# Gate and up projections: four instead of three of the eight step pairs by Strassen's scheme, with three buffers for the pre-added weights and three load slots

## What is computed

```
h2 = rms_norm(x, g_ffn[i])
x = x + (jax.nn.silu(h2 @ w_gate[i]) * (h2 @ w_up[i])) @ w_down[i]
```

## Time and profile before

| | |
|---|---|
| median of 3 runs | 2746.8 us (2746.69 to 2747.99) |
| the profiled execution | 2746.42 us |
| its span in the trace | 2744.6 us |
| PE / PEld busy | 99% / 83% of the span |
| DVE / ACT / POOL busy | 67% / 51% / 4% |
| pairs of gate and up | 11, between about 1930 us and 2573 us of the span |

### The profile page before, as it was taken

The page is one execution under the profiler, slowest core; times in us unless marked ns, Lnnn a source line. Parts: engine busy times, 40 slices in busy tenths (PEclk is TensorE's granted clock), DMA queues, the critical chain, the costliest instruction groups (busy, mean ns, idle before and its releaser), DMA issues.

```text
span 2744.6 us, 31158 instructions
## 1 busy us (share of the span) xinstructions
PE 2730.5 (99%) x12990; PEld 2269.2 (83%) x12990; DVE 1842.4 (67%) x1666; ACT 1405.0 (51%) x1532; POOL 110.3 (4%) x160
## 2 busy tenths in 40 slices
PE   9999999999999999999999999999999999999999
PEld 7888778888888888888888888888888888888887
DVE  5445765455468878878788685665787478658665
ACT  5435664345566556455465545344654355445553
POOL 0000000000000000000000000000121021001000
PEclk9999999999999999999999999999999999999999
DMA  7745036655545555555555664546888588768555
GB/s 235 224 148 169 32 108 200 199 184 199 175 163 206 193 199 179 204 197 193 209 185 183 225 197 145 183 156 204 257 266 252 176 252 247 246 192 255 196 182 171
DMA packets 235645, 534.16 MB, mean 195 GB/s; under 512 B 11683, under 2 KB 22513, under 8 KB 234609
## 3 DMA queue, kind: packets, MB, share of 16 engines
q1 hardware_dynamic: 218528, 486.97, 52.7%
q0 software_dynamic: 16800, 44.97, 6.7%
q10 hardware_dynamic: 176, 0.23, 0.0%
HBM read 530.03 MB, written 2.10 MB: 194 GB/s over the span
## 4 chain that ended last, share of the span: by engine, by line
PE 87%; DVE 1%; ACT 1%; DMA 0%; issue 0%
PE acc L876 13%; PE acc L877 13%; PE acc L881 13%; PE acc L1359 7%; PE acc L1360 7%; PE acc L1364 7%; PE tb L1364 7%; PE tb L1359 7%; PE tb L1360 7%; PE tb L1349 1%; PE tb L861 1%; PE acc L1142 0%; PE tb L1193 0%; ACT prob L1935 0%; PE acc L1084 0%; PE acc L1081 0%
## 5 line engine op out<-in xcount | busy, mean ns | idle before, releaser
L2326 DVE TENSOR_TENSOR wlo<-raw,whi 128x2048 fp32r<-128x2048 f32 (+2 forms) x465 | 1024.0, 2212 | 586.2 <-ACT whi L1692 585.4
L1692 ACT ACTIVATE whi<-raw 128x2048 fp32r<-128x2048 f32 (+2 forms) x465 | 858.4, 1853 | 607.9 <-PE acc L881 300.8
L876 PE MATMUL acc<-whi,ahi 128*128 128x512 f32 (+1 forms) x1456 | 566.6, 390 | 0.4 <-DVE alo L2441 0.4
L877 PE MATMUL acc<-whi,alo 128*128 128x512 f32 (+1 forms) x1456 | 562.2, 387 | 0.0
L881 PE MATMUL acc<-wlo,ahi 128*128 128x512 f32 (+1 forms) x1456 | 357.7, 387 | 0.0
L876 PEld LDWEIGHTS acc<-whi,ahi 128*128 128x128 f32 x1456 | 274.0, 188 | 55.6 <-DVE wlo L2438 0.9
L877 PEld LDWEIGHTS acc<-whi,alo 128*128 128x128 f32 x1456 | 274.1, 188 | 54.4
L881 PEld LDWEIGHTS acc<-wlo,ahi 128*128 128x128 f32 x1456 | 271.0, 188 | 55.5
L1359 PE MATMUL acc<-whi,ff_hi 128*128 128x512 f32 x512 | 201.6, 394 | 0.2 <-DVE h L2404 0.2
L1360 PE MATMUL acc<-whi,ff_lo 128*128 128x512 f32 x512 | 199.7, 390 | 0.0
L1706 ACT ACTIVATE whi<-tsum 128x1024 fp32r<-128x1024 f32 x97 | 103.1, 1062 | 182.5 <-DVE tsum L2337 122.5
(11 more groups left out here) (414 smaller groups left out, 3782.1 us busy)
## 6 DMA issues: line engine op xcount, KB each, us to landing
raw<-in_w_ff SPq DMA_DIRECT2D x128, 1024.0 KB, 5.0
raw<-in_w_in SPq DMA_DIRECT2D x119, 1024.0 KB, 5.1
raw<-in_w_gate SPq DMA_DIRECT2D x88, 512.0 KB, 4.7
raw<-in_w_down SPq DMA_DIRECT2D x44, 1024.0 KB, 5.3
raw<-in_w_up SPq DMA_DIRECT2D x55, 512.0 KB, 6.8
tpre<-in_w_up POOLq DMA_DIRECT2D x99, 256.0 KB, 5.9
raw<-in_w_out SPq DMA_DIRECT2D x16, 1024.0 KB, 5.2
raw<-in_w_o SPq DMA_DIRECT2D x16, 1024.0 KB, 5.1
```

What stands on the lines that cost most here:

```text
L876: nc.tensor.matmul(out_(t), hi[:, kt, tt(t)], whi[:, slot, wc(k)], start=first and k == 0, stop=False)
L877: nc.tensor.matmul(out_(t), lo[:, kt, tt(t)], whi[:, slot, wc(k)], start=False, stop=False)
L1692: nc.scalar.activation(whi[:, g % SPLIT, 0:n_], raw_of(n)[:, 0:n_], ACT.Copy).then_inc(w_hi, 1)
L2326: V.tensor_tensor(wlo[:, g % SPLIT, 0:n_], raw_of(load_of(g))[:, 0:n_], whi[:, g % SPLIT, 0:n_].bitcast(F32), ALU.subtract).then_inc(w_lo, 1)
```

## The change

The plan of a pair becomes D D S S D S S D. The items are then D0 D1 B2 T3 B4 T5 D6 B7 T8 B9 T10 D11. The places of the two transposes stay at steps 4 and 6, now ahead of D6 and of B9. The buffers `tpre` become three; the third one takes the place of load slot 4, so the loads have slots 0, 1 and 3. POOL's order becomes: copies of sums 0 and 1; then for each n: wait for the copies of n, the two accumulating transfers of n, and then, when the buffer is free (`wlo` of sum n-1, which used it), the copies of n+2. Each buffer gets a semaphore pair of its own.

```diff
-FF1_PLAN, FF2_PLAN, GUD_PLAN = "DDSDDSDD", "DDSDDSDD", "DDSDSDSD"
+FF1_PLAN, FF2_PLAN, GUD_PLAN = "DDSDDSDD", "DDSDDSDD", "DDSSDSSD"
...
-            double(GUD_PLAN, (0, 1, 3, 4), 2)
+            double(GUD_PLAN, (0, 1, 3), 2)
         mark["gud_end"] = len(kinds)
-        plain(4 * pairs, (0, 1) if n == len(GUD_PAIRS) - 1 else (0, 1, 3, 4))
+        plain(4 * pairs, (0, 1) if n == len(GUD_PAIRS) - 1 else (0, 1, 3))
...
-        tpre = [sb("tpre0", [P, 2, COLS], F32, W_AT + 8 * KB), sb("tpre1", [P, 2, COLS], F32, B_AT + 27 * KB)]
+        tpre = [sb("tpre0", [P, 2, COLS], F32, W_AT + 8 * KB), sb("tpre1", [P, 2, COLS], F32, B_AT + 27 * KB),
+                sb("tpre2", [P, 2, COLS], F32, W_AT + 50 * KB)]
...
-                            if n >= 2:
-                                pool.wait_ge(w_lo, SUM_ITEM[GUD_SUMS + n - 2] + 1)
-                            pool.dma_start(into[:, 0, :], wu[:, 2 * step, at]).then_inc(pre_in, 16)
-                            pool.dma_start(into[:, 1, :], wg[:, 2 * step + 1, at]).then_inc(pre_in, 16)
-                            pool.wait_ge(pre_in, 32 * (n + 1))
-                            for k in range(2):
-                                pool.dma_start(into[:, k, :], wu[:, 2 * step + 1, at], accum_op=ALU.add
-                                               ).then_inc(pre_sum, 16)
...
+                def copied(n):
+
+                    at, step = steps[n]
+                    if n >= 3:
+                        pool.wait_ge(w_lo, SUM_ITEM[GUD_SUMS + n - 3] + 1)
+                    pool.dma_start(tpre[n % 3][:, 0, :], wu[:, 2 * step, at]).then_inc(pre_in[n % 3], 16)
+                    pool.dma_start(tpre[n % 3][:, 1, :], wg[:, 2 * step + 1, at]).then_inc(pre_in[n % 3], 16)
+
+                copied(0)
+                copied(1)
+                for n, (at, step) in enumerate(steps):
+                    pool.wait_ge(pre_in[n % 3], 32 * (n // 3 + 1))
+                    for k in range(2):
+                        pool.dma_start(tpre[n % 3][:, k, :], wu[:, 2 * step + 1, at], accum_op=ALU.add
+                                       ).then_inc(pre_sum[n % 3], 16)
+                    if n + 2 < len(steps):
+                        copied(n + 2)
```

More of the change, by code:

```diff
@@ L501, in build @@
         mm_half, w_hi_half = sem("mm_half"), sem("w_hi_half")
-        pre_in, pre_sum = sem("pre_in"), sem("pre_sum")
+        pre_in, pre_sum = ([sem(f"{name}{n}") for n in range(3)] for name in ("pre_in", "pre_sum"))
         t_sum, t_hi, f_in, f_sum = sem("t_sum"), sem("t_hi"), sem("f_in"), sem("f_sum")
@@ L827, in _ @@
                 pool.wait_ge(mm_done, MARK["gud"] - 3)
[L828 to L833, removed]
-                            if n >= 2:
-                                pool.wait_ge(w_lo, SUM_ITEM[GUD_SUMS + n - 2] + 1)
-                            pool.dma_start(into[:, 0, :], wu[:, 2 * step, at]).then_inc(pre_in, 16)
-                            pool.dma_start(into[:, 1, :], wg[:, 2 * step + 1, at]).then_inc(pre_in, 16)
-                            pool.wait_ge(pre_in, 32 * (n + 1))
-                            for k in range(2):
-                                pool.dma_start(into[:, k, :], wu[:, 2 * step + 1, at], accum_op=ALU.add
-                                               ).then_inc(pre_sum, 16)
-                            n += 1
+                wg, wu = ktiles(a["w_gate_2"]), ktiles(a["w_up_2"])
+                steps = [(slice(c * COLS, (c + 1) * COLS), step) for c in range(sum(GUD_PAIRS))
+                         for step, kind in enumerate(GUD_PLAN) if kind == "S"]
+                def copied(n):
[13 more added lines that the diff above has]
+                        copied(n + 2)
                 pool.wait_ge(w_lo, MARK["gud_end"])
@@ L1701, in sums_hi @@
                         act.wait_ge(mm_done, g + 1 - SPLIT)
-                        act.wait_ge(pre_sum, 32 * (m + 1))
-                        src = tpre[m % 2][:, :, :].rearrange("p k n -> p (k n)")
+                        act.wait_ge(pre_sum[m % 3], 32 * (m // 3 + 1))
+                        src = tpre[m % 3][:, :, :].rearrange("p k n -> p (k n)")
                     else:
@@ L2334, in weight_sums @@
                 m = n - GUD_SUMS
-                pre = t[:, 0:2 * COLS] if m < 0 else tpre[m % 2][:, :, :].rearrange("p k n -> p (k n)")
+                pre = t[:, 0:2 * COLS] if m < 0 else tpre[m % 3][:, :, :].rearrange("p k n -> p (k n)")
                 if m < 0:
@@ L2341, in weight_sums @@
                 else:
-                    dve.wait_ge(pre_sum, 32 * (m + 1))
+                    dve.wait_ge(pre_sum[m % 3], 32 * (m // 3 + 1))
                     V.tensor_tensor(t[:, col(2)], pre[:, col(1)], r[:, col(1)], ALU.add).then_inc(t_sum, 1)
```

## The result

The changed kernel took 2756.3 us (median of 6 runs, 2751.35 to 2759.08), the kernel before 2747.4 in the same session (2746.69 to 2748.44). The ratio is 1.0032 [1.0022, 1.0042]: slower by 0.32%, or 8.9 us. I had forecast 2740.8. The time lies inside the range, on the other side of no change.

What follows compares the result with a forecast made beforehand. PE alone, busy for 99% of the span, was taken to set the time. From the median 2746.8 us, -7.5 for fewer matmuls and +1.5 for the first pair gave -6.0: 2740.8 us, range 2739.0 to 2757.

Steps and rivals of the forecast that it cites:

- PE's gain: One D becomes an S in each of 11 pairs: 33 matmuls less at 0.227, 7.5 us saved.
- Loads with three slots: Load of the next pair's D1: 8.7 us allowed, 9.6 in the earlier trace; a loss of 0.9 a pair or none.
- rival 2: D1's load late by 0.3 to 0.9 in eight pairs: 2743.2 to 2748.0 us; chance 0.30 together with Rival 4.
- Last step: D11, a pair's last step: `wlo` done at 36.65, needed at 36.7; no loss taken, or 0.1 to 0.3 in eight pairs.
- The walk: Step-by-step timing of ACT and DVE through one pair against PE's needs; slacks of 1.1, 1.3 and under 0.1 us.
- The first pair: Activation tiles among its weights make T5, T10 and D11 late: between nothing and 3.9 us, 1.5 taken.
- The sums by transfer: POOL's copies and accumulations for T10 land by 29.1, DVE wants them at 29.5: covered by 0.4 us.
- Rival 4: Third buffer does nothing, accumulations waiting behind copies; 0.6 a pair if 1 us later; chance 0.30 together with rival 2.
- What the transfers cost: DMA in a pair: 39.7 us needed of 41.77, 95%; 276 GB/s wanted against 281 at a share of 0.97.
- rival 3: Transfers become the bound in every pair: 0.8 to 1.2 more each, +8 to +15, 2755 to 2762 us; chance 0.30.
- a pair over 42.45 throughout: Sign: pairs that all last longer than the 42.45 us of before would mark rival 3.
- rival 2 or 3: Sign: PE waiting for the folds L2831 or L2834 would mean one of these two, a late load of D1.

Runs made afterwards that it cites:

- e10: e2 with PE making four instead of two matmuls in a pair's last step before the first one with `wlo`; 2741.35 us, ratio 0.9977.
- e1: Changed kernel with DVE making a pair's last two folds ahead of the `wlo` of the next pair's D1; 2743.92 us, ratio 0.9988.
- e2: Changed kernel with four load slots again and all three `tpre` buffers, the third in two separate halves; 2744.01 us, ratio 0.9989.
- e7: Changed kernel whose accumulating transfers add only 64 of the 512 columns; 2744.19 us, ratio 0.9986.
- e9: e1 with PE making four instead of two matmuls in a pair's last step before the first one with `wlo`; 2741.54 us, ratio 0.9980.
- e11: Kernel before with PE making four instead of two matmuls in a pair's last step before the first one with `wlo`; 2748.09 us, ratio 1.0002.
- e4: Kernel before with only the new plan: two buffers, four load slots, POOL's old order; 2793.93 us, ratio 1.0176.

## Why the prediction was wrong

**PE's gain: right.** -7.5 us from 33 matmuls at 0.227. With both waits removed (e10) a pair lasts 41.80, where 41.77 was forecast, and 6.4 of the 7.5 us arrive.

**"Loads with three slots": the step that failed.** It found the place (the slot freed by T10's sum, L2831 behind D1's `wlo`), the allowance of 8.7 us, and a landing of 9.6 in the earlier trace rows; the sum then took no loss for it, and rival 2 took at most 0.9 a pair. Measured from issue to ACT's start in the eight places: 7.5 to 10.9 us, over 8.7 in five. PE waited in six of eight, 0.24 to 2.02 us, 7.4 in all; with restarts and slow matmuls 10.6. Two things were left out. The one landing in the earlier trace rows was taken as the bad end, though the plan changes what flies beside the load: now copies and accumulations for the S steps of the next pair. And the price of a wait was taken as its own length alone. Shown by e1 (the order alone), e2 (the slot alone) and e7 (the accumulations alone).

**"Last step. Slack under 0.1 ... I take 0": mis-sized.** The walk said 0, or 0.1 to 0.3 if its sums were short. It measured 0.28 a pair (0.17 of waiting and 0.11 at the restart), 3.1 us in 11: DVE started that `wlo` 1.72 us before PE's step in e2, where the walk had 1.95 (36.3 less 34.35); e9 and e10 give 2.6 and 2.9 of it back, and e11 shows that the old plan had slack there.

**"The first pair": mis-sized the other way.** 1.5 us were taken. From its first matmul to its bank copy it lasted 36.95 us, against 37.46 before; less three matmuls that would be 36.78, so under 0.2 was lost to there, and its last step waited 0.36 longer than the others: some 0.5 in place of 1.5.

**The sums by transfer: right.** ACT waited for `tpre` four times, 3.8 us in all, and PE never for a T step's `whi`. POOL's order works against its own look-ahead as described, yet the 0.4 us of cover held well enough. Rival 4 fell with it; e4 shows what the buffer does: 37.6 us with this plan.

**What the transfers cost: the load was right, the limit was not.** 95% was forecast; the pair of e10 shows a share of 0.94. But 281 GB/s at 0.97 was no ceiling: 322, 340 and 348 GB/s stand in the windows above, at shares of 1.00 to 1.07. The trace of the kernel before had shown it, in windows that the prediction did not read:

```profile
1925.00:1935.00 10.00, 10.00 (x44) 7.99 (x43) 6.64 (x4) 3.38 (x3) 1.77 (x2) 1.00 1.06 362
1965.00:1975.00 10.00, 10.00 (x46) 8.26 (x45) 9.86 (x7) 6.69 (x7) 1.81 (x3) 1.00 1.04 346
```

The Trainium skill, "DMA: Bandwidth & Descriptors", section Specifications, puts HBM's limit for a core at about 358 GB/s. Of the windows shown here one is just past it and the others are under it, so the page's figure is nearer than my reading of the row.

**The rivals.** The time, +8.9, is that of rival 3 at its small end, but its mechanism fell: e1, e2 and e10 carry the same transfers at full speed. The place was rival 2's, at most 7.2 us there and 10.6 here. A number that fits is not a mechanism that holds. In the signs, a pair over 42.45 throughout was to mark rival 3; the pairs lasted 42.08 to 46.00 (from PE's last step to the next pair's), shortest where the load came in time, and PE's wait stood at L2839, which the text had given to "rival 2 or 3" and so could not have told them apart.

**Left open:** what part of the landing time is the copies' and what the accumulations' queueing (e7 makes only the latter small), and why the clock was lower from 180 to 195 us in the profiled execution of the changed kernel.

## What to carry to other kernels

When a buffer is bought with a load slot, ask when the next load is issued now, what flies beside it then, and, above all, what stands behind its consumer on that engine: a late load costs nothing until something that the bounding engine needs is queued behind it. Put short work that frees a resource ahead of work that waits for a transfer, and keep a wait of the bounding engine as late in its order as the data allow. If a step's slack comes out at 0.1 us by a sum of ten rows, price it as lost, once for each repetition; and before work is moved away from a chain, check whether the same work was cover on the other side.

## What the runs showed of the hardware

- A PE wait of 2.02 us was followed by eight matmuls 0.43 us apart; one of 1.77 us was not (first two rows, the changed kernel). The length alone does not decide: in e4 a wait of 2.05 us was followed by seven such matmuls, and one of 2.87 us by none (last rows):

```profile
1977.68 0.39 PE L1372 MATMUL acc<-wlo,gud_hi 128*128 128x512 f32 x1
1979.84 0.50 PE L1367 MATMUL tb<-whi,gud_hi 128*128 128x512 f32 x1 [1.77 <-DVE gud_e L2839]
...
2106.67 0.50 PE L1359 MATMUL acc<-whi,gud_hi 128*128 128x512 f32 x1 [2.87 <-ACT whi L1706]
2107.00 0.39 PE L1360 MATMUL acc<-whi,gud_lo 128*128 128x512 f32 x1
...
2606.01 0.50 PE L1359 MATMUL acc<-whi,gud_hi 128*128 128x512 f32 x1 [2.05 <-ACT whi L1706]
...
2607.33 0.63 PE L1359 MATMUL acc<-whi,gud_hi 128*128 128x512 f32 x1
2607.76 0.63 PE L1360 MATMUL acc<-whi,gud_lo 128*128 128x512 f32 x1
```

- The same 1 MiB load took at most 6.0 us from issue to use beside small accumulations (e7, in the eight places), and 7.5 to 10.9 beside full ones in the changed kernel.
- 16 DMA engines moved 340 GB/s over 10 us in the changed kernel and 348 in e2, while a window at a share of 0.97 in the kernel before had 281, and another at 1.06 had 362: a share near 1 did not mean that no more could be moved.
